# Merging the two scan directions in a bidirectional RWKV-7 / windowed-attention block, and moving its softmax one block back

## What is computed

```python
    def step(S, inp):
        rt, wt, kt, vt, at, bt = inp
        Sa = jnp.einsum('zbhij,zbhj->zbhi', S, at)
        S = S * wt[..., None, :] + Sa[..., :, None] * bt[..., None, :] + vt[..., :, None] * kt[..., None, :]
        return S, jnp.einsum('zbhij,zbhj->zbhi', S, rt)
    _, ys = lax.scan(step, S0, xs)            # z: the two directions
    y = (ys[:, 0] + ys[::-1, 1]).transpose(1, 0, 2, 3)
...
    s = jnp.einsum('bnqhgd,bnkhd->bnhgqk', qb, kb).astype(f32) * (D ** -0.5)
    s = s - slopes[:, :, None, None] * dist.astype(f32)
    sink_col = jnp.broadcast_to(sink..., s.shape[:-1] + (1,))
    p = jax.nn.softmax(jnp.concatenate([s, sink_col], axis=-1), axis=-1)[..., :-1]
    o = jnp.einsum('bnhgqk,bnkhd->bnqhgd', p.astype(v.dtype), vb)
```

## Time and profile before

| | us |
|---|---|
| median of 3 runs | 1472.81 (1465.94 to 1473.66) |
| the profiled execution | 1464.1 |
| its span, first to last instruction | 1462.3 |
| PE busy | 1333.3 (91% of the span) |
| DVE, ACT, POOL busy | 876.9, 558.6, 169.4 |
| chain that ended last: share of PE, DVE, ACT, DMA | 71%, 13%, 6%, 4% |

### The profile page before, as it was taken

The page is one execution under the profiler, slowest core; times in us unless marked ns, Lnnn a source line. Parts: engine busy times, 40 slices in busy tenths (PEclk is TensorE's granted clock), DMA queues, the critical chain, the costliest instruction groups (busy, mean ns, idle before and its releaser), DMA issues.

```text
span 1462.3 us, 28521 instructions
## 1 busy us (share of the span) xinstructions
PE 1333.3 (91%) x11292; PEld 1055.2 (72%) x11292; DVE 876.9 (60%) x1151; ACT 558.6 (38%) x825; POOL 169.4 (12%) x165
## 2 busy tenths in 40 slices
PE   6999899995898998878969999999999998999996
PEld 2476676773776776647857788888888887888885
DVE  4977667886565676755248655565555573233235
ACT  3725525310565666672125333333333341121121
POOL 1000100120010000021100422222222200000000
PEclk9999999996899998999979999999999999999998
DMA  5046756874466585510410222222222246322113
GB/s 200 19 123 170 188 148 171 203 226 106 150 226 196 178 242 154 164 62 29 172 58 0 87 87 86 86 86 86 86 86 71 81 177 227 105 87 97 43 33 115
DMA packets 154788, 179.52 MB, mean 123 GB/s; under 512 B 61648, under 2 KB 117008, under 8 KB 154736
## 3 DMA queue, kind: packets, MB, share of 16 engines
q1 hardware_dynamic: 141568, 152.69, 35.4%
q10 hardware_dynamic: 9264, 14.19, 3.0%
q0 software_dynamic: 3904, 11.93, 2.6%
HBM read 121.16 MB, written 57.54 MB: 122 GB/s over the span
## 4 chain that ended last, share of the span: by engine, by line
PE 71%; DVE 13%; ACT 6%; DMA 4%; issue 3%; POOL 1%; ACTq 1%; SPq 0%; DVEq 0%; POOLq 0%
PE banks L1053 26%; PE banks L678 16%; PE banks L660 7%; PE banks L1088 4%; PE banks L666 3%; DMA work<-in_w_in 2%; PE banks L914 2%; PE banks L904 2%; DVE work L1827 2%; DVE work L1823 2%; ACT work L1286 1%; PE banks L642 1%; PE banks L937 1%; PE banks L872 1%; PE banks L883 1%
## 5 line engine op out<-in xcount | busy, mean ns | idle before, releaser
L1053 PE MATMUL banks<-op,sw_hi 128*128 128x512 f32 x1176 | 364.1, 391 | 5.4 <-DVE hT L2009 4.3
L1053 PEld LDWEIGHTS banks<-op,sw_hi 128*128 128x128 f32 x1176 | 221.6, 189 | 52.8 <-DVE sw_lo L1622 5.3
L1053 PE MATMUL banks<-op,sw_lo 128*128 128x512 f32 x588 | 229.5, 390 | 0.0
L1959 DVE TENSOR_TENSOR xT<-xT,banks 128x1024 f32<-128x1024 f32 x24 | 29.3, 1221 | 169.7 <-PE banks L678 156.8
L1053 PEld LDWEIGHTS banks<-op,sw_lo 128*128 128x128 f32 x588 | 110.9, 189 | 23.1
L1396 ACT ACTIVATE sw_hi<-work 128x1024 fp32r<-128x1024 f32 (+1 forms) x63 | 75.9, 1205 | 122.5 <-PE banks L1053 113.0
L1622 DVE TENSOR_TENSOR sw_lo<-work,sw_hi 128x1024 fp32r<-128x1024 f32 (+1 forms) x63 | 90.1, 1430 | 39.4 <-ACT sw_hi L1396 39.3
L660 PE MATMUL banks<-ph_hi,pw_hi 128*128 128x512 f32 x272 | 88.5, 408 | 6.9 <-DVE pw_lo L1622 3.3
L660 PE MATMUL banks<-ph_hi,pw_lo 128*128 128x512 f32 x272 | 86.5, 400 | 0.0
L678 PE MATMUL banks<-g_hi,down_hi 128*128 128x512 f32 x256 | 80.0, 394 | 4.0 <-DVE g_lo L1622 3.5
L678 PE MATMUL banks<-g_hi,down_lo 128*128 128x512 f32 x256 | 79.7, 393 | 0.0
(11 more groups left out here) (246 smaller groups left out, 2492.3 us busy)
## 6 DMA issues: line engine op xcount, KB each, us to landing
work<-scan_d SPq DMA_DIRECT2D x32, 768.0 KB, 4.9
work<-in_w_gu SPq DMA_DIRECT2D x88, 256.0 KB, 4.5
scan_d<-work SPq DMA_DIRECT2D x16, 1024.0 KB, 5.4
g_d<-hT SPq DMA_DIRECT2D x22, 512.0 KB, 2.9
scan_d<-work SPq DMA_DIRECT2D x32, 256.0 KB, 6.4
work<-in_w_down SPq DMA_DIRECT2D x16, 512.0 KB, 3.8
work<-in_w_in ACTq DMA_DIRECT2D x15, 512.0 KB, 3.8
work<-g_d SPq DMA_DIRECT2D x15, 512.0 KB, 4.5
```

The source lines that it names most:

```text
L1053: mm = pe.matmul(banks[:, 3 * slot + bank, :], w[:, n, k * P:(k + 1) * P], x[n][:, k, :], start=(opens and k == 0 and p_ == 0), stop=(k == ...
L1959: tt(x, x, product, ALU.add).then_inc(added[slot], 1)
```

## The change

1. In L904, L937, L952 and L962 the loop over the directions moves inside the loop over head pairs. Of any four matmuls in a row, each now uses another of four tiles of the array (row half x column half); before, eight pairs on two of the tiles came first and eight pairs on the other two after them. L914 keeps its order, since both directions' state lies in the same rows.
2. The two directions' copies and state updates become one instruction each of double width: `U_low`, `U_high`, `Y_out`, `S_add`, `S_new`. The semaphores of each direction become one, except those of `Xs`.
3. `XY` and `US` swap banks from step to step, so L904 waits for the previous `S_add`, no longer for `Y_out`; L937 waits for `Y_out`.
4. The softmax is cut up. Logits are made one head at a time (heads 0, 1, 2 in the even step, 3 in the odd one), the maximum in two halves, exponentials and normalisation in pieces between the copies.
5. Transposes and values come one block later: in the odd step of group `g` of iteration `i`, PE works on block (i-1, g), not on the block before. They are cut up too: transposes 0 and 1, then L937, transpose 2 and the first part of the values, then L952, L962 and the rest of the values.
6. SP: `load_values(i - 1)` stands at the head of iteration `i`, where `load_values(i)` stood behind the second step's stores. The distances are loaded apart from queries and keys. Behind the scan there are two blocks left to transpose and multiply, where there was one.

```diff
             def chunk_steps(i, lead):
...
-                    for z in range(2):
-                        c2 = cc if z == 0 else 1 - cc
-                        pe.wait_ge(sz[z]["Y_out"], n + FREE)
-                        for j in range(NPAIR):
+                    c2s = (cc, 1 - cc)
+                    XY = [banks[:, 2 * cc + z, 0:NPAIR * HD] for z in range(2)]
+                    US = [banks[:, 2 - 2 * cc + z, :] for z in range(2)]
+                    pe.wait_ge(s["S_add"], n + FREE)
+                    for j in range(NPAIR):
+                        for z, c2 in enumerate(c2s):
                             for e in range(2):
...
-                    elif behind:
-                        probabilities(*before, 8 * i + 4 * g + 4)
+                    elif not lead:
+                        probabilities(i - 1, g, scored, (0, 1))
...
-                    elif behind:
-                        values(*before)
+                    elif not lead:
+                        probabilities(i - 1, g, scored, (2,))
+                        values(i - 1, g, (0,), scored)
+                    pe.wait_ge(s["U_low"], n + 1)
+                    pe.wait_ge(s["U_high"], n + 1)
...
+                    if cc == 1 and not lead:
+                        values(i - 1, g, (1, 2), scored)
...
             for first, last in ((0, 1), (1, YT - 1), (YT - 1, NC // 4 - 1)):
                 with sp.Fori(first, last) as i:
                     for slot in range(2):
                         if slot == 1:
+                            sp.wait_ge(s["sc_mm"], 8 * i + 8)
+                            load_qk(i + 1)
+                        elif last > 1:
+                            sp.wait_ge(s["o_mm"], 2 * i - 2 + FREE)
+                            load_values(i - 1)
+                        store_y(i, 2 * slot)
+                        if slot == 1:
                             sp.wait_ge(s["sc_out"], 8 * i + 8)
-                            load_qk(i + 1)
-                        store_y(i, 2 * slot)
+                            load_distances(i + 1)
                         store_y(i, 2 * slot + 1)
-                        if slot == 0 and last > 1:
-                            sp.wait_ge(s["o_mm"], 2 * i + FREE)
-                            load_values(i)
...
# ACT, in each step
+                        act.wait_ge(X_mm[1], n + 1)
+                        act.activation(Xs[:, 1], banks[:, 2 * cc + 1, 0:256], ACT.Copy).then_inc(X_out[1], 1)
+                        if cc == 0 and earlier:
+                            exponentials(blk - 1, 1 - g, (1,))
+                        if cc == 1 and first:
+                            transposed(blk - 2, (0, 1))
...
+                        if cc == 0 and earlier:
+                            normalised(blk - 1, 1 - g, (0,))
+                        if cc == 1 and earlier:
+                            normalised(blk - 1, 1 - g, (3,))
+                        if cc == 1 and first:
+                            attended(i - 1, g)
+                        if cc == 1:
+                            exponentials(blk, g, (0,))
...
# DVE, in each step
-                        for z in range(2):
-                            c = n if z == 0 else (i * -4 + (NC - 1 - q))
-                            dve.wait_ge(sz[z]["S_mm"], n + 1)
-                            tt(St[:, z], S[:, z], banks[:, 2 + z, 256:512].rearrange("p (j i) -> p j i", j=NPAIR), ALU.add)\
+                        dve.wait_ge(s["S_mm"], n + 1)
+                        tt(St[:, :, :, :], S[:, :, :, :], banks[:, 2 - 2 * cc:4 - 2 * cc, 256:512]
...
+                        if cc == 0:
+                            logits(i, g, (2,), earlier)
+                            if earlier:
+                                sums(blk - 1)
+                        else:
+                            maxima(i, g)
```

More of the change, by code:

```diff
@@ L282, in hymba_block, with u_rows @@
         qs, ks, vs, nd = w(4, P), w(2, BAND), w(3, P), w(BAND)
+        def u_rows(slot, rows, cc):
+            return UV[slot].rearrange("p z c j i -> p (z c) (j i)")[rows, cc:4 - cc:3 - 2 * cc, :]
         yn = oT[:, 0:NPAIR, :].rearrange("p j (n c) -> p j n c", c=P)
@@ L849, in _, with scores @@
             mm.then_inc(s["vat_mm"], 1)
-            XY = [banks[:, z, 0:NPAIR * HD] for z in range(2)]
-            US = [banks[:, 2 + z, :] for z in range(2)]
-            def scores(i, g, heads, behind):
+            def scores(i, g, heads, later):
                 blk = 2 * i + g
@@ L857, in scores, with probabilities @@
                     e, hh = h % 2, h // 2
-                    if behind and h == heads[0]:
-                        pe.wait_ge(s["pt_out"], 3 * blk - 3 + FREE)
-                    if behind and h == GH - 1:
-                        pe.wait_ge(s["o_out"], blk - 1 + FREE)
+                    if later and h == GH - 1:
+                        pe.wait_ge(s["o_out"], blk - 2 + FREE)
                     pe.matmul(banks[:, 4 + h, 0:BAND], qs[64 * e:64 * e + 64, 2 * g + hh, :],
                               ks[64 * e:64 * e + 64, g, :], start=True, stop=True).then_inc(s["sc_mm"], 1)
-            def probabilities(i, g, scored):
+            def probabilities(i, g, scored, parts):
                 pe.wait_ge(s["p_norm"], 2 * i + g + 1)
-                pe.wait_ge(s["sc_out"], scored)
-                for kb in range(3):
+                for kb in parts:
+                    pe.wait_ge(s["sc_out"], scored + kb - 3)
                     for h in range(GH):
@@ L891, in chunk_steps @@
                     n = 4 * i + q
-                    behind = not (lead and g == 0)
-                    before = (i, 0) if g else (i - 1, 1)
+                    scored = 8 * i + 4 * g + 4
+                    c2s = (cc, 1 - cc)
+                    XY = [banks[:, 2 * cc + z, 0:NPAIR * HD] for z in range(2)]
+                    US = [banks[:, 2 - 2 * cc + z, :] for z in range(2)]
                     if lead and q == 0:
@@ L906, in chunk_steps @@
                                           start=(j == 0), stop=False, skip_group_check=True)
-                    for z in range(2):
-                        c2 = cc if z == 0 else 1 - cc
-                        pe.wait_ge(sz[z]["S_new"], n + 1)
-                        settled()
+                    pe.wait_ge(s["S_new"], n + 1)
+                    settled()
+                    for z, c2 in enumerate(c2s):
                         for j in range(NPAIR):
@@ new lines, in chunk_steps @@
+                        scores(i, g, (0, 1), not lead)
+                    elif not lead:
+                        probabilities(i - 1, g, scored, (0, 1))
+                    if lead and q == 0:
+                        pe.wait_ge(scan_full[0], 16 * 10)
+                        pe.wait_ge(s["lw_full"], 16 * (NPAIR + 6))
+                        pe.wait_ge(s["q_stored2"], 16 * 10)
+                    for z in range(2):
+                        pe.wait_ge(X_out[z], n + 1)
+                    pe.wait_ge(s["Y_out"], n + FREE)
@@ L938, in chunk_steps @@
                                                Xs[hu, z, j * HD:(j + 1) * HD], start=True, stop=True)
-                        mm.then_inc(sz[z]["U_mm"], 1)
+                    mm.then_inc(s["U_mm"], 1)
                     if cc == 0:
-                        scores(i, g, (2, 3), behind)
-                    elif behind:
-                        values(*before)
-                    for z in range(2):
-                        c2 = cc if z == 0 else 1 - cc
-                        pe.wait_ge(sz[z]["U_e0"], n + 1)
-                        pe.wait_ge(sz[z]["U_e1"], n + 1)
-                        settled()
-                        for j in range(NPAIR):
+                        scores(i, g, (2, 3), not lead)
+                    elif not lead:
+                        probabilities(i - 1, g, scored, (2,))
+                        values(i - 1, g, (0,), scored)
@@ L955, in chunk_steps @@
                                                start=True, stop=True)
-                        mm.then_inc(sz[z]["S_mm"], 1)
-                    for z in range(2):
-                        c2 = cc if z == 0 else 1 - cc
-                        for j in range(NPAIR):
+                    mm.then_inc(s["S_mm"], 1)
+                    for j in range(NPAIR):
+                        for z, c2 in enumerate(c2s):
                             for e in range(2):
```

224 lines of the change are left out of this document (114 added, 110 removed).

## The result

The changed kernel takes **1478.1 us** (median of 10 runs, 1469.7 to 1481.4), the kernel before 1470.4 (median of 10, 1465.9 to 1473.7). The ratio is 1.0043, with a 95% interval of 1.0025 to 1.0062. So it is slower by 0.4%; the forecast was 0.2% faster.

The account below looks back on a forecast made before the run. PE's own queue was taken as the bound in undisturbed iterations (28.02 of 29.40 us). Terms -10.6 + 8.6 - 4.4 + 4 = -2.4 us on the profiled 1464.1 gave 1461.7, 1470 us as a median; range 1447 to 1486.

Parts of the forecast that it names:

- The groups of 32 records: PE's scan products: a group on four tiles takes 0.56 us instead of about 0.9, saving 5.4 us per iteration.
- If nothing else waited, an iteration would take 23.8 us: Scan iteration without other waits: two even steps of 5.5 us and two odd of 6.4, against 29.4 before.
- The values come late: Step 1 of each iteration: values land at 11.6 us, PE needs them at 9.2 and waits 2.4 us.
- Iterations 1 to 4: -10.6: Early scan: iterations 1, 3 and 4 gain 3.2 us each, iteration 2, with the `xT` transfers, gains 1.
- The clock: PE's granted clock after new waits in iterations 1 to 7: 0.5 us per short wait, 0.7 per long, +4 us.
- rival B: Scan: the clock drops after every wait, costing 13 to 30 us instead of 4; 1487 us, chance 0.20.
- The first iteration: Its last three steps, without transposes, take 20 us instead of 24.40: -4.4 us.
- Iterations 5 to 7: Late scan: the output read-back delays the values, PE waits 6.8 and twice 4.8 us; +8.6 us together.
- Rival A: Scan: the values land in time, so short and long waits shrink and the clock's loss goes; 1449 us, chance 0.23.
- C: Scan products: four tiles run no faster than two, groups stay at 0.9 us; +10, 1483 us, chance 0.04.

Follow-up runs that it names:

- two tiles: Changed kernel with the direction loop outermost again in the four products that had been merged pair by pair: 1495.2 us, ratio 1.0161.
- Values first: Changed kernel with each block pair's values loaded at the end of iteration i, ahead of slot 1's ten DMAs: 1451.2 us, ratio 0.9876.
- both loads moved: Changed kernel with values loaded ahead of slot 1's ten DMAs and POOL's `xT` loads issued in the first iteration: 1444.4 us, ratio 0.9828.
- the split loop: Kernel with both loads moved and ACT's late square one step later (1435.3 us), PE's loop written as two, iteration 1 and 2 to 7: 1436.7 us, one run.
- The filled waits: Changed kernel with idle PE transposes ahead of the values' wait: 16 per iteration, 1478.6 us; 36 in each iteration's second step only, 1468.9 us, one run.
- `xT` early: POOL's eight `xT` loads issued in the first iteration: changed kernel 1475.3 us, ratio 1.0034; kernel before 1458.1 us, ratio 0.9929.

## Why the prediction was wrong

**The groups of 32 records: right.** I took 0.56 us and expected 0.55 to 0.65; they take 0.58 to 0.63, and two tiles give 0.83 to 0.91. The rule that I had weighed against this (the Trainium skill, "TensorE: Matmul & The Clock Gate", section "Wait — 56ns, not 53.3ns?") gives 0.80 us for 32; the trace does not agree with it. DVE's merged copy and addition, taken as 0.66 us, take 0.67 to 0.69 by themselves.

**"If nothing else waited, an iteration would take 23.8 us": 1.3 too low.** Values first showed 25.1. The even step is 5.58 us for my 5.5; the odd one is 6.98 for 6.4, because the groups are 0.02 to 0.07 longer each, the cut-off pieces of transposes and values 0.05 to 0.09, and a gap of 0.22 for DVE's multiplication comes in ahead of L923. (The gap of 0.22 ahead of L914, for the addition, lies in the even step.)

**"The values come late": right in place, time and length, except in iterations 1 and 2.** Issue at 7.9 us after the start (7.7 taken), landing 3.9 us later (3.9), waits of 2.2 and 2.8 us in iterations 3 and 4 (2.4), 5.5, 4.2 and 5.1 in the late ones (6.8, 4.8, 4.8). Iteration 1, for which I took 2.4 too, has no such wait, and iteration 2 has one of 12.1.

**"Iterations 1 to 4: -10.6": the step that failed; it was +5.2.** The overlap in iteration 2 and the path of iteration 1 were wrong. This is where the sign was lost, 15.8 us of it:

- Iteration 2, -1 taken, +4.1 measured. I said that its length was set by what the DMA engines carry, and did not put the values' DMA, issued at 429.64, behind the eight transfers of 420.18. In the kernel before PE waits 5.55 us for a slot there; now it waits 12.1 for the values. The place of the values is only a part: with values first PE waits for the slot again and the iteration still takes 38.2 us, and only with both loads moved it takes 25.5. Here the transfers of `xT` hold up both loads that come behind them.
- Iteration 1, -3.2 taken, +2.9 measured: PE has no wait for the values and less work at full clock, but a granted clock of 0.76 for 0.95 and the stop of 3.1 us. Values first leaves it at 34.1 us. The stop had no row in the kernel before, whose longest in that place was 0.7. By the split loop, run once, it belongs to a first pass. Why the clock was lower is open; it was near the lower level before the iteration began (0.55 from 381 to 391).
- Iterations 3 and 4, -3.2 taken, -0.5 and -1.4 measured: 1.3 each by the undisturbed length, 1.6 in iteration 3 by the clock behind its wait.

**The clock: +4 taken, a size too small.** Behind the six waits the same step was longer than its work and its wait together by 2.3, 1.6, 0.1, 2.3, 2.3 and 2.3 us: 10.9, or 1.8 each, and the steps that follow the four long ones take 1.2 to 2.3 us more than the undisturbed 5.58. I had set 1.3 us per wait as the point from which rival B turns the sum; by my own terms it is 0.9, since the sum without the clock was -6.4 and I counted seven waits. B's mechanism is there behind five waits of six, at a smaller price than its 14 us, and its 1487 us are 9 above what was measured, as the forecast's 1470 are 8 below. The filled waits show that not all of it can be had back: with the clock kept, the next step's waits take more than half.

**The first iteration: -4.4 taken, -2.1 measured.** PE's busy time there fell from 21.89 to 18.26 us in a stretch that the chain sets, and the granted clock from 0.86 to 0.65. Another 4.6 us came from the stretches ahead of it (2.5 in the scan's start, 2.1 in the first step), for which I had nothing; the scan's start differs by as much between kernels that are alike there (the kernel before started its scan at 340.6, and with `xT` early, which is the same up to there, at 337.6), so I don't count it as an effect.

**Iterations 5 to 7: +8.6 taken, +9.3 measured**, right by luck. The 8.6 were without the clock; of the 9.3, 6.9 are the clock behind the three waits, which leaves 2.4. And I had measured iteration 6 from an undisturbed 34.7 us, where the trace of before, from which the sum starts, has 38.9. One by one: iteration 5 +4.4 for +1.7, iteration 6 -1.1 for +2.2, iteration 7 with what follows +5.9 for +4.7. The waits were shorter than taken and the clock (0.81, 0.79) worse.

With -10.6 replaced by +5.2 and the late term by +9.3, both with their clock, and the first iteration by -2.1, the sum is +12.3 (before rounding); the 4.6 us ahead of it and 2.1 from the gate products on, where I had expected nothing, leave +5.6, the difference of the spans. With the clock kept as a term of its own, the miss of 8.0 us is +11.8 in iterations 1 to 4, +6.9 in the clock, +2.3 in the first iteration, -6.2 in the late ones and -6.7 in stretches for which I had nothing: two large errors one way, and two the other way that hid more than half of them.

Rival A did not occur. I gave it 1449 us, and values first, which puts the values in time in all iterations but one, runs at 1451; that the price fits is partly luck, since the clock's loss did not go with the waits (0.80 in iterations 5 and 6). C did not occur, and its price of 1483 us was too low: with two tiles the kernel takes 1495.

## What to carry to other kernels

A change that makes a queue's consumer faster has to be walked with every transfer in that iteration, not in the undisturbed one alone: here 192 KB issued behind 4 MB made PE wait 12 us in one iteration, and the whole change gives 4 in an undisturbed one. When an edit moves a small load that the next step needs, put it ahead of the bulk loads of its queue; that one move turned +0.4% into -1.2%. A shorter step on one engine may gain nothing as long as a piece of side work on another is longer than its gaps, as the logits of 2.17 us were, and the gain is measured in an iteration that nothing disturbs.

## What was not expected of the hardware

- Transfers of 16 KB on the instruction queue q8 appear in a loop's first pass only: in the changed kernel eleven from 340 to 425 us and none from there to 640, and five more in the kernel whose second loop is made of the same code. Beside them PE stops without a releaser: up to 3.1 us in the changed kernel, 0.7 in the one before, though both have eleven transfers. Where `xT` is loaded at the same time the stops reach 3.1 to 4.1 us in the first iteration (2.2 in the kernel before, in iteration 1). Not every such stop is one of these: one of 1.3 us stands in iteration 7 of the changed kernel with `xT` early, without a transfer.
- Behind a wait of 2.2 us in iteration 3 the mean granted clock was 0.61 for 4.3 us (473.24 to 477.57), behind one of 2.8 us in iteration 4 it was 1.00. Behind waits of 4.2 to 5.5 us PE worked at the lower level for the rest of the step and a part of the next (0.50 from 533.0 to 541.5).
- The same DMA of 192 KB lands in 2.4 us ahead of ten others, 3.9 behind them, 5.1 behind these and a read-back of 1 MB, and 12.4 behind 4 MB.
